# A deeper LayerNorm routine with feed-forward parts between its steps, small inputs loaded first, casts moved

## The reference, cut to what matters

```python
u = _ln_plain(x) * (1.0 + sc1) + sh1
mix, st = _token_mixer(u, ...)            # projections, short conv, RG-LRU scan, two gated branches, w_o
x = _ln(DN_ALPHA * x + g1 * mix, ln1_g[l], ln1_b[l])
u2 = _ln_plain(x) * (1.0 + sc2) + sh2
f = _swiglu(u2, ...) if l % 2 == 0 else _moe(u2, ...)   # dense in layer 0, top 2 of 8 experts in layer 1
x = _ln(DN_ALPHA * x + g2 * f, ln2_g[l], ln2_b[l])
```

## Time and profile before

| | us |
|---|---|
| median of 3 runs | 2567.03 |
| lowest, highest | 2563.63, 2713.2 |
| profiled execution | 2563.05 |
| its span on the slowest core (core 3) | 2561.4 |
| spans of the other cores | 2495.4 to 2516.6 |
| TensorE busy (span of core 3) | 1908.2 (74%) |
| VectorE busy | 1234.9 (48%) |
| ScalarE busy | 795.6 (31%) |
| GpSimd busy | 186.5 (7%) |

### The profile page before, as it was taken

One profiled execution on the slowest core, in us unless ns is written; L12 is line 12 of the kernel. 1 busy time (PEld: TensorE's weight loads), 2 busy tenths in 40 slices (PEclk: granted clock), 3 DMA queues, 4 the chain that ended last, 5 costly groups with the idle time before them and its releaser, 6 DMA issues.

```text
span 2561.4 us, 31864 instructions; the slowest of 8 cores (2495.4 to 2561.4 us)
## 1 busy us (share of the span) xinstructions
PE 1908.2 (74%) x11218; PEld 1031.4 (40%) x11218; DVE 1234.9 (48%) x1687; ACT 795.6 (31%) x1192; POOL 186.5 (7%) x257
## 2 busy tenths in 40 slices
PE   0488889957898863498899841787899879499940
PEld 0244445423454422244445311455445545254520
DVE  0379972375335165398953496122232222133259
ACT  0688881124111123398841111211111111111100
POOL 1010000000000100001000002100000000000030
PEclk9999999977998986799999975898999989799975
DMA  8468776432399999999998405699898999666753
GB/s 181 68 92 119 112 121 136 75 44 42 50 127 145 135 144 143 124 169 179 179 189 129 73 1 112 169 230 207 192 205 194 220 219 211 130 130 129 195 165 131
DMA packets 93864, 359.56 MB, mean 140 GB/s; under 512 B 6464, under 2 KB 6976, under 8 KB 87488
## 3 DMA queue, kind: packets, MB, share of 16 engines
q0 software_dynamic: 63568, 240.71, 61.0%
q1 hardware_dynamic: 26736, 102.93, 12.2%
q10 hardware_dynamic: 3328, 13.11, 1.3%
HBM read 539.67 MB, written 92.36 MB: 247 GB/s over the span
## 4 chain that ended last, share of the span: by engine, by line
PE 61%; DMA 14%; DVE 11%; issue 7%; ACT 5%; POOL 1%; SPq 0%; DVEq 0%; ACTq 0%; POOLq 0%; PEldq 0%
PE ps L182 61%; DMA s_big<-moe_f 5%; DVE s_big L182 3%; DVE s_xres L182 3%; DMA s_big<-ffn_f 3%; ACT s_ubuf L182 2%; DVE s_tw L182 2%; DMA s_condt<-cond 2%; DVE s_mv L182 2%; DMA s_big<-w_p 1%; DMA s_big<-xs 1%; ACT s_xres L182 1%; ACT s_big L182 1%; DMA xsv<-s_xres 1%; POOL xs L185 1%
## 5 line engine op out<-in xcount | busy, mean ns | idle before, releaser
L182 PE MATMUL ps<-s_ubuf,s_big 128*128 128x512 bf16 (+5 forms) x6912 | 1196.8, 336 | 112.7 <-issue 44.1
L182 PEld LDWEIGHTS ps<-s_ubuf,s_big 128*128 128x128 bf16 x6912 | 674.9, 100 | 625.0 <-issue 179.1
L182 PE MATMUL ps<-s_big 128*128 128x512 bf16 (+1 forms) x2820 | 633.1, 382 | 180.0 <-DVE s_tw L182 81.2
L182 DVE TENSOR_TENSOR s_big<-ps,s_big 128x256 bf16<-128x256 f32 (+8 forms) x421 | 286.0, 682 | 797.0 <-PE ps L182 791.9
L182 PEld LDWEIGHTS ps<-s_big 128*128 128x128 bf16 x2820 | 281.8, 101 | 518.0 <-issue 255.2
L182 ACT ACTIVATE s_big<-ps 128x512 f32<-128x512 f32 (+5 forms) x342 | 165.9, 490 | 769.7 <-PE ps L182 705.4
L182 ACT ACT_TABLE_LOAD x85 | 109.1, 1283 | 320.9 <-PE ps L182 148.0
L182 ACT ACTIVATE s_tw<-ps 128x512 f32<-128x512 f32 (+1 forms) x175 | 91.7, 546 | 345.5 <-PE ps L182 342.7
L182 DVE SCALAR_TENSOR_TENSOR s_big<-s_big,s_smallp 128x1260 f32<-128x1260 f32 (+1 forms) x80 | 122.0, 1525 | 7.1 <-ACT s_big L182 0.4
L185 POOL DMA_DIRECT2D s_big<-moe_f x72 | 51.8, 720 | 947.5 <-PE ps L182 730.6
L182 DVE TENSOR_TENSOR s_big<-ps,s_tw 128x512 f32<-128x512 f32 (+3 forms) x96 | 55.2, 598 | 116.3 <-PE ps L182 116.3
(11 more groups left out here) (93 smaller groups left out, 931.0 us busy)
## 6 DMA issues: line engine op xcount, KB each, us to landing
pc<-moe_f POOLq DMA_DIRECT2D x48, 1024.0 KB, 37.5
s_big<-pc SPq DMA_DIRECT2D x48, 1024.0 KB, 11.4
s_big<-moe_f POOLq DMA_DIRECT2D x48, 1024.0 KB, 21.1
s_big<-moe_f POOLq DMA_DIRECT2D x24, 1536.0 KB, 17.5
s_big<-w_p POOLq DMA_DIRECT2D x32, 1024.0 KB, 17.3
s_big<-w_mod POOLq DMA_DIRECT2D x24, 1024.0 KB, 19.2
s_big<-ffn_f POOLq DMA_DIRECT2D x12, 1024.0 KB, 22.2
ys<-s_tw SPq DMA_DIRECT2D x1, 10240.0 KB, 202.5
```

What stands on the lines that cost most here:

```text
L182: getattr(eng, name)(*a, **kw).then_inc(sems[e], 1)
```

## The change

The order of the six small loads and the three loads of x is swapped, with `cond` first. The first norm works one step ahead: it uses `xnbf` and the region `tmA` in turn, three pairs of PSUM banks, takes the statistics of pair s before the end of pair s-1 and the transposes of pair s-2, and gives every second scale-and-shift operation to VectorE (`split`). The four modulation products now stand behind the statistics of the second pair, followed by four casts.

`tail` runs over seven steps instead of five: `resid` and the first statistics of pair s, then `norm` of pair s-1, then `fin` and `turn` of pair s-2. The parts of the feed-forward are cut by weight piece: (0,0) and (0,1) stand in step 4, (0,2) in step 5, all of tile 1 in step 6 ahead of the last `turn`, tile 2 behind it. The banks are no longer reserved. The loop at the end of the kernel takes the statistics of pair s before `affine` of pair s-1.

Casts in the order of the code, before: 8 in p1 of layer 0, 2 at the output weights, 12 in quarters 1 and 2 of the feed-forward, 12 behind its last weights, 8 in p1 and 4 in p2 of layer 1, 2 at the output weights. After: 4 at the start, 8 in p1 of layer 0, 4 in p2, 8 behind the output weights, 6 in the feed-forward's first parts, 3 in quarter 1, 4 in p2 of layer 1, 11 behind its output weights.

```diff
@@ -527,12 +527,12 @@
+        for ii, (dst, src, key) in enumerate([(condt, cond_d, 'cond'), (smallp, smallp_d, 'smallp'), (identf, ident_d, 'identf'),
+                                              (flg, flg_d, 'flg'), (h0t, h0_d, 'h0'), (rcon, rconst_d, 'rcon')]):
+            P.dma('sp', 'lds%d' % ii, lambda e, dst=dst, src=src: e.dma_start(out=dst[:], in_=src), writes=[key])
         for j, (t0, tn) in enumerate(TILES):
...
-        for ii, (dst, src, key) in enumerate([(smallp, smallp_d, 'smallp'), (flg, flg_d, 'flg'), (h0t, h0_d, 'h0'),
-                                              (condt, cond_d, 'cond'), (identf, ident_d, 'identf'), (rcon, rconst_d, 'rcon')]):
-            P.dma('sp', 'lds%d' % ii, lambda e, dst=dst, src=src: e.dma_start(out=dst[:], in_=src), writes=[key])
...
@@ -582,13 +582,12 @@
-        def affine(tbs):
-            m = moments(tbs, 1)
+        def affine(tbs, m):
...
-        def plain(tbs):
+        def plain(tbs, xb=xnbf, xk=(('xnbf', 0), ('xnbf', 1))):
...
@@ -597,23 +596,28 @@
                 for i, tb in enumerate(tbs):
-                    act(lambda e, tb=tb, i=i: e.activation(out=xnbf[:, i * D:(i + 1) * D], in_=xres[:, tb, :], func=AF.Identity,
-                                                           scale=rs[:, 2 + i:3 + i], bias=rs[:, 4 + i:5 + i]), [('x', tb), rk], [('xnbf', i)])
+                    act(lambda e, tb=tb, i=i: e.activation(out=xb[:, i * D:(i + 1) * D], in_=xres[:, tb, :], func=AF.Identity,
+                                                           scale=rs[:, 2 + i:3 + i], bias=rs[:, 4 + i:5 + i]), [('x', tb), rk], [xk[i]])
...
-        def turn_u(l, p, shc, scc):
+        def turn_u(l, p, shc, scc, xb=xnbf, xk=(('xnbf', 0), ('xnbf', 1)), b=6, split=False):
...
             for i in range(2):
                 for c in range(NCH):
-                    pe(lambda e, c=c, i=i: e.transpose(out=psb[:, 6 + i, c * 128:(c + 1) * 128], in_=xnbf[:, i * D + c * 128:i * D + (c + 1) * 128],
-                                                       identity=identb[:]), [('xnbf', i), 'identb'], pk(6 + i))
+                    pe(lambda e, c=c, i=i: e.transpose(out=psb[:, b + i, c * 128:(c + 1) * 128], in_=xb[:, i * D + c * 128:i * D + (c + 1) * 128],
+                                                       identity=identb[:]), [xk[i], 'identb'], pk(b + i))
             for c in range(NCH):
...
-                act(lambda e, c=c, s1=s1, s2=s2: e.activation(out=ubuf[:, c, p * 256:(p + 1) * 256].rearrange("p (a b) -> p a b", a=2),
-                                                              in_=psb[:, 6:8, c * 128:(c + 1) * 128], func=AF.Identity, scale=s1, bias=s2),
-                    pk(6, 2) + [('modT', l)], keys)
+                dst = ubuf[:, c, p * 256:(p + 1) * 256].rearrange("p (a b) -> p a b", a=2)
+                src = psb[:, b:b + 2, c * 128:(c + 1) * 128]
+                if split and c % 2:
+                    dve(lambda e, dst=dst, src=src, s1=s1, s2=s2: e.tensor_scalar(out=dst, in0=src, scalar1=s1, scalar2=s2, op0=ALU.mult, op1=ALU.add),
+                        pk(b, 2) + [('modT', l)], keys)
+                else:
+                    act(lambda e, dst=dst, src=src, s1=s1, s2=s2: e.activation(out=dst, in_=src, func=AF.Identity, scale=s1, bias=s2),
+                        pk(b, 2) + [('modT', l)], keys)
...
@@ -649,9 +653,9 @@
-        def tail(mm, resid, norm, turn, mid=None, late=None):
+        def tail(mm, resid, norm, turn, ffn=None):
...
-            fin = None
+            m, fin = {}, {}
...
@@ -659,25 +663,27 @@
-            for p in range(5):
-                for tb in (2 * p, 2 * p + 1):
-                    resid(tb, 2 * (tb % 3))
-                fill(2 * p + 5)
-                if fin:
-                    fin()
-                if p:
-                    turn(p - 1)
-                fin = norm([2 * p, 2 * p + 1])
-                if p == 3 and mid:
-                    pst['reserved'] = {0, 1, 4, 5}
-                    mid()
-                    pst['reserved'] = set()
-            fin()
-            if late:
-                late(1)
-            turn(4)
-            if late:
-                late(2)
+            for s in range(7):
+                if s < 5:
+                    for tb in (2 * s, 2 * s + 1):
+                        resid(tb, 2 * (tb % 3))
+                    m[s] = moments([2 * s, 2 * s + 1], 1)
+                    fill(2 * s + 5)
+                if ffn and s == 4:
+                    ffn(0, 0)
+                if 1 <= s <= 5:
+                    fin[s - 1] = norm([2 * s - 2, 2 * s - 1], m[s - 1])
+                if ffn and s in (4, 5):
+                    ffn(0, s - 3)
+                if s >= 2:
+                    fin[s - 2]()
+                    if ffn and s == 6:
+                        for n in range(3):
+                            ffn(1, n)
+                    turn(s - 2)
+            if ffn:
+                for n in range(3):
+                    ffn(2, n)
...
@@ -926,18 +932,22 @@
-            for p in range(5):
-                tbs = [2 * p, 2 * p + 1]
-                g = p // 4
-                for tb in tbs:
+            m = {}
+            for s in range(6):
+                for tb in (2 * s, 2 * s + 1) if s < 5 else ():
+                    g = tb // 8
...
-                affine(tbs)
-                for tb in tbs:
-                    tk = P.dma('sp', 'sty', lambda e, tb=tb: e.dma_start(out=yout[tb * 128:(tb + 1) * 128, :], in_=xres[:, tb, :]), reads=[('x', tb)])
-                    out_toks.append(tk)
+                if s < 5:
+                    m[s] = moments([2 * s, 2 * s + 1], 1)
+                if s:
+                    tbs = [2 * s - 2, 2 * s - 1]
+                    affine(tbs, m[s - 1])
+                    for tb in tbs:
+                        tk = P.dma('sp', 'sty', lambda e, tb=tb: e.dma_start(out=yout[tb * 128:(tb + 1) * 128, :], in_=xres[:, tb, :]), reads=[('x', tb)])
+                        out_toks.append(tk)
...
@@ -974,13 +984,13 @@
-        def ffn_first(l, j):
+        def ffn_first(l, j, n):
             if j == 0:
-                mod_job(l + 1, 0)
-                for n in range(3):
-                    ffn_q0.append(ring_next(('f1', l, 0, 0, 2 * n), hold=n))
-            for n in range(3):
-                ffn1(0, 2 * n, ffn_q0[n][0], ffn_q0[n][1], [j])
+                if n == 0:
+                    mod_job(l + 1, 0)
+                ffn_q0.append(ring_next(('f1', l, 0, 0, 2 * n), hold=n))
+                precast(2)
+            ffn1(0, 2 * n, ffn_q0[n][0], ffn_q0[n][1], [j])
...
@@ -992,7 +1002,8 @@
                     for i in range(0, 6, 2):
...
-                        precast(2)
+                        if q == 1:
+                            precast(1)
...
@@ -1012,10 +1023,9 @@
-            precast(12)
-
-            def norm(tbs):
-                affine(tbs)
+
+            def norm(tbs, m):
+                affine(tbs, m)
                 for tb in tbs:
...
@@ -1028,7 +1038,7 @@
-        TWK = ['gbc', ('lnbc', 0), ('lnbc', 1), 'tmA']
+        TWK = ['gbc', ('lnbc', 0), ('lnbc', 1), 'tmA', 'tmA1']
...
@@ -1058,16 +1068,23 @@
-        for n in range(4):
-            mod_job(0, n)
-
...
                 if l == 0:
-                    for p in range(5):
-                        plain([2 * p, 2 * p + 1])()
-                        turn_u(l, p, 0, 8)
+                    XB = [(xnbf, (('xnbf', 0), ('xnbf', 1))), (tmA.bitcast(BF16), ('tmA', 'tmA1'))]
+                    fin = {}
+                    for s in range(7):
+                        if s < 5:
+                            fin[s] = plain([2 * s, 2 * s + 1], *XB[s % 2])
+                        if 1 <= s <= 5:
+                            fin[s - 1]()
+                        if s == 1:
+                            for n in range(4):
+                                mod_job(0, n)
+                            precast(4)
+                        if s >= 2:
+                            turn_u(l, s - 2, 0, 8, *XB[s % 2], 2 + 2 * (s % 3), True)
...
@@ -1099,7 +1116,8 @@
-                    precast(1)
+                    if l == 0:
+                        precast(1)
...
@@ -1279,7 +1297,7 @@
                 def x_part(m):
...
-                    if l and m % 2:
+                    if m % 2:
...
@@ -1324,8 +1342,8 @@
                 for h in range(2):
...
-                    precast(4 if l else 1)
...
+                precast(NE * NPRE if l else 8)
...
@@ -1346,19 +1364,19 @@
-                    def norm_m(tbs):
-                        affine(tbs)
+                    def norm_m(tbs, m):
+                        affine(tbs, m)
...
-                    def norm_d(tbs):
-                        affine(tbs)
+                    def norm_d(tbs, m):
+                        affine(tbs, m)
...
-                    tail(mm, resid, norm_d, lambda p: turn_u(l, p, 24, 32), lambda: ffn_first(l, 0), lambda j: ffn_first(l, j))
```

(1 more changed line is left out.)

## The result

| | before | changed |
|---|---|---|
| median, us | 2567.03 | 2471.77 (4 runs, 2468.9 to 2478.43) |
| profiled execution | 2563.05 | 2471.3 |
| span of core 3, the slowest | 2561.4 | 2469.6 |
| ratio of times | | 0.9639, interval 0.9604 to 0.9674 |

The account below looks back on a forecast made before the run. It took TensorE, nearly full in the projections, to be badly filled in five places. Terms -34 + 2 - 6 - 19 - 13 - 32 - 1 = -103 from 2563.1 gave 2460, 2462 for the median; range 2438 to 2502.

Parts of the forecast that it names:

- likeliest rival: Start gains little: x and modulation weights slow each other, or pairs keep to 9.4 us; about 2490, 9 in 100.
- Part 1: Start and first LayerNorm: vectors land first, pairs pipeline at 5.3 us, first projection at 74.4 instead of 108.3; -34 us.
- Pairs 0 and 1 are normalised as soon as x is there: First LayerNorm: these pairs no longer wait for the conditioning vectors; first statistics expected at 13 to 17 us.
- ScalarE sets the pace or nearly: First LayerNorm: ScalarE's 5.3 us a pair, against VectorE's 5.2, sets the pipeline's period.
- The casts of the start: Four casts behind the first weights delay chunk 2's weight in layer 0's first projection; +2 us, bounds 0 and +10.
- Part 2: Layer 0's mixer LayerNorm: one pair deeper, no square root waited for, 16 us a pair; -6 us, bounds +6 and -14.
- Part 3: Casts moved out of the feed-forward's weights end its three waits and half-rate matmuls; -19 us, bounds -8 and -24.
- Part 4: LayerNorm after the feed-forward runs at VectorE's 16 us a pair; next projection starts at 997.7; -13 us, bounds -6 and -20.
- late next in the feed-forward: With weight waits gone, VectorE's evictions, busy 33.9 of 38 us, were to limit the feed-forward next.
- Part 5: Layer 1's first projection: without casts at the barrier on x, the 30.8 us wait for chunk 1's weight goes; -32 us.
- The rest: Layer 1's LayerNorm loses only its first table-load wait, -1 us; the final LayerNorm 0, bounds -2 and +2.
- The rival on the slow side: Casts ahead of weights in POOL's full queue cost 7.2 us for each weight pushed past need; 2620, 3 in 100.

Follow-up runs that it names:

- e1: Changed kernel with the first x tile's load issued second on SP's queue, behind the conditioning vectors: median 2473.5 us, ratio 0.9669.
- e4: Changed kernel with the edits of e1, e2 and e3 together: median 2471.7 us, ratio 0.967; first projection starts at 68.2 us.
- e2: Changed kernel with a PSUM bank each for ScalarE's and VectorE's scale-and-shift in the first LayerNorm: median 2468.7 us, ratio 0.9649.
- e3: Changed kernel with the previous pair's normalisation issued ahead of this pair's statistics in the first LayerNorm: median 2470.2 us, ratio 0.9648.
- e9: e4 without the four casts of the start, which move to the feed-forward's third part and layer 1: median 2453.9 us, ratio 0.9583.
- e5: Changed kernel run again, nothing edited: 2471.2 and 2481.0 us, no ratio; first `tail` stretch 162.4 us.
- e7: Changed kernel with the LayerNorm routine of before, start and casts staying changed: median 2498.5 us, ratio 0.9734.
- e6: Changed kernel with the feed-forward products of the first two tiles behind the last pair's normalisation: median 2483.8 us, ratio 0.9657.
- e10: e9 with the feed-forward products of the first two tiles behind the LayerNorm's last pair, as in e6: 2455.2 and 2460.0 us, no ratio.
- e12: Kernel before the change with only the new places of all casts: median 2517.7 us, ratio 0.9831.
- e11: Changed kernel with twelve of layer 1's casts back behind the feed-forward's last weights: median 2508.9 us, ratio 0.98.
- e8: Changed kernel with all 48 casts at their old places, start and LayerNorm routine staying changed: median 2550.8 us, ratio 0.9923.

## Why the prediction was right or wrong

Faster, and by the named steps; the measured 2471.8 lies 10 above the forecast and inside the range. The likeliest rival was also partly true: "a pair keeps to 9.4 us instead of 5.3" (it gave 2490 for losing 20 to 34; 12 were lost). That the total came so near is partly luck: in the profiled execution the first `tail` was 9.1 us worse than its forecast, by that execution's clock, and the last stretch 8.2 better, and the two cancel.

**Part 1, the start: -22 instead of -34.** This is the step that failed: a pair was to take 5.3 us and took 10.0. With 12 us it is, net, the whole shortfall. "Pairs 0 and 1 are normalised as soon as x is there": true, but x came at 34.0, not at 13 to 17; by e1 that alone cost 2. "ScalarE sets the pace or nearly" added up each engine's work as if the two ran side by side; in the changed kernel they ran one after the other. The durations were right: VectorE's scale-and-shift takes 0.41 us (taken: 0.5, bounds next to nothing and 0.65), and e4 runs at 4.9. What was not read was the order: which bank both read (e2: 14.5 us), and what stands ahead of what on ScalarE (e3: 7.2). The start landed outside the part's own bounds, -26 to -38, since the bounds came from durations alone.

**The casts of the start: +2, measured 0**, for a start at 86.6, and within the scatter of that stretch. This term was too small as well, though the late start hid it. The weight of chunk 2 was to land at 126. In e2 and e4, where TensorE is ready before it, the modulation weight lands at 127.6 and 126.7 and the projection's at 133.7 and 132.8, though the two start 3.9 us apart. TensorE's waits for weights are 14.5 us at a start of 68.2 (e4), 12.3 at 72.1 (e2), 0.9 at 79.4 (e3), and none without these casts (e9). For the start that I forecast, 74.4, I estimate some 10 us from e2's 12.3, the term's upper bound. So the right start alone would have won back only a part of its 12 us: at the end of p2 e2 is 9.4 us ahead of the changed kernel and e4 3.0, but e9 18.9. A gain ahead of a full queue and the queue's backlog are one term, not two.

**Part 2: -6, measured -5.5** (e5; e7 -5.7). Behind it the steps hold too: a pair takes 15.8 to 16.0 us (forecast 16), its waits ahead of affine(3) are 7.2 (forecast about 8), and the last tile ends at 641.0, 27.7 ahead of the earlier trace rows, of which 22.2 are the start's. The first profile's +3.1 was the granted clock of that execution, 0.73; eight other executions of this routine took 162.0 to 165.0 us. The table switches behaved as the earlier trace rows and not as the rule of the Trainium skill (ScalarE: Activation LUTs, What ACT_TABLE_LOAD costs) had it; ScalarE in e5:

```profile
579.54 5.17 ACT L182 ACTIVATE s_ubuf<-ps,s_modT 128x256 bf16<-128x256 bf16 x8 [1.25 <-PE ps L182]
584.73 1.28 ACT L182 ACT_TABLE_LOAD   x1
586.03 0.30 ACT L182 ACTIVATE s_rs<-s_mv,s_epsc 128x2 f32<-128x2 f32 x1
586.34 1.28 ACT L182 ACT_TABLE_LOAD   x1
587.63 0.60 ACT L182 ACTIVATE s_big<-ps 128x512 f32<-128x512 f32 x1
```

0.02 and 0.01 us after a load the next operation runs, and the loads themselves start 0.02 and 0.01 us after the operation before them. By that rule the part would have gained 3; it gained 5.5. The parts in between are no part of the gain: without them the stretch is 3.3 us shorter in e6 and 1.4 in e10.

**Part 3: -19, measured -20.8** (e12: 9.9 and 10.9). **Part 4: -13, measured -12.0** (e7). Together -34.8 in e5, forecast -32. What was said to be late next in the feed-forward, VectorE, is busy for 30.3 of 34 us there, and TensorE 31.8.

**Part 5: -32, measured -24 to -30.** The stall of 30.8 is gone, in both executions. The stretch shrank by 30.4 in one and 24.4 in the other, for the same 2083 matmuls took 356.9 and 362.5 us of TensorE at a granted clock of 0.96 and 0.95. The cause named, casts in the queue when the barrier opens, is shown by e11.

**The rest.** Third `tail` and routing: -0.2 and -0.7, forecast -1, which can't be told from none. The last stretch, 4 to 8 shorter, was not forecast; it moves by 18 us between kernels that don't touch it, and what moves it stays open.

The rival on the slow side (a cast for each weight pushed past its need) came nearest to life in e4, where p1 and p2 took 15.5 us more with the four casts, not in the changed kernel.

## What to carry to other kernels

To forecast a pipeline over two engines, write out each engine's queue in its strict order for one full period, with every cross-engine wait between its items, PSUM banks read by both among them; sums per engine give only a floor. Background transfers in a queue that is full are free only as long as the work behind them is late: when the work ahead is sped up, move them in the same edit (e4 gave 0, e9 gave 18 us). And read a small change by its own stretch, in two executions at least, since a granted clock or an untouched stage can move a total by as much.

## What the runs showed of the hardware

- 2 MB of x issued on SP's queue at 3.8 us, beside 4 MB of modulation weights that POOL issued from 2.8 to 5.7, landed in 28.8 to 30.1 us (changed kernel, e2, e3). Issued at 1.1 to 1.5 us, ahead of them, it landed in 11.0 to 11.7 (before, e1, e4).
- For the same 568 matmuls of one stretch TensorE's granted clock was 0.73 in one execution and 0.82 in another, and TensorE was busy for 132.5 and 119.2 us; in 24 us of it the clock was 0.77 and 0.99 at an equal DMA share.
- Two engines that scale from a PSUM bank each take 1.95 us (VectorE) and 2.52 us (ScalarE) for four operations each, side by side (e4). Where the kernel's own tracking makes them take turns on shared banks, eight took 4.6.
- With twelve casts in the queue a weight issued 38.8 us earlier landed only 18.3 us earlier (e8 against before).
